# Scan in two buffers, zeros behind the weight chunks, and twelve of the modulation's parts moved from the scan into the context's attention

## The chip, the cores and the metric
The kernel runs on one core of a Trainium2 chip. The metric is the device time of one execution in microseconds. Engines are named PE (TensorE), VectorE (DVE), ScalarE (ACT), GpSimd (POOL) and SyncE (SP, which issues most DMAs).

## The reference
Two layers of a transformer block on 256 context and 256 latent tokens of width 1024, in float32. Cut to what matters here:

```python
for i in range(2):
    mod_x = split((silu(c) @ w_mod[i] + b_mod[i]), 6)      # shift, scale, gate: twice
    mod_c = split((silu(c_ctx) @ w_mod[i] + b_mod[i]), 6)
    u = concat([ada_norm(hc, g, mod_c[0], mod_c[1]), ada_norm(hx, g, mod_x[0], mod_x[1])])
    proj = u @ w_in[i]
    o_da  = diff_attention_mixer(proj[...])   # 4 heads, two softmaxes each, RoPE on the latent tokens
    o_ssd = ssd_mixer(proj[...])              # conv, chunked scan in both directions, gate, norm
    o_mla = mla_mixer(proj[...])              # 4 heads
    mix = concat([o_da, o_ssd, o_mla]) @ w_out[i]
    hc, hx = hc + mod_c[2] * mix_c, hx + mod_x[2] * mix_x
    ... # moe_ffn: 16 experts, top 2 of one group; hx and (in layer 0) hc are updated
return rms_norm(hx, final_norm_g)
```

A chunk of the scan (128 tokens) computes, for each direction and head, `y = ((C B^T) * exp(a_cum_i - a_cum_j) * mask) @ (x * dt) + exp(a_cum) * (C @ state)`, and adds `d_skip * x`.

## The kernel before, in words
Each engine runs one program of its own, in the order written, and the engines meet at semaphores. All loops over layers, tiles and heads are unrolled; only the expert loop is a loop on the chip. A tile is 128 tokens: tiles 0 and 1 are context, 2 and 3 latent. In layer 1 only tiles 2 and 3 go through scan and attention.

PE's order in a layer is: norm, input projection, states of the scan, rotation (RoPE), `scan_tiles`, `attention`, `out_projection`, router, experts. VectorE, ScalarE and GpSimd follow the same order.

`scan_tiles` before, for each tile i: PE multiplies C and B (`cb`, L612); GpSimd builds rows (`ew`, L1786), and PE spreads them over the partitions by a product with ones (L622, the cast) into PSUM banks 2 and 3, one direction after the other; VectorE subtracts and clamps (L1150, eight small operations, the clamp); ScalarE takes the exp (L1582); GpSimd multiplies by the masked scores (L1804), having made x*dt (L1792) and d_skip*x (L1797) for the tile; PE sums (L634 and L640) into banks 4 to 6; VectorE adds up and gates y (L1163 to L1174, the y chain); ScalarE takes its square and the root (L1584, L1510, L1511); VectorE norms it (L1182), PE transposes it (L402) and VectorE copies it out (L1187). `ew` is one buffer for each direction, so GpSimd builds the rows of a tile only when PE has summed the tile before (L1785).

The modulation is cut into 30 parts: for each of two layers three groups, in each four products with a chunk of w_mod of 2 MB (L424) and one part that turns the result (L402 on `modrow`). A part is placed wherever PE's program says `spare(n)`; VectorE has the same calls at its own places. Five parts run before the projections, five in the rotation and 20 in layer 0's scan (five for each tile: two behind each cast and one at the end). Bank 7 holds their sums. The chunks come through a ring of four slots of 2 MB in SBUF, together with w_in and w_out; SP loads a slot once its last user has released it (L1834). The order is: group 0, w_in's five, groups 1 to 5, w_out's two, then the experts' weights.

The experts' rows go through a DRAM tensor, `slots`, which must be zero before tokens are scattered into it. SP writes the zeros with four DMAs of 6 MB (L1898), before it loads w_in's chunk for z.

`attention` runs over units (kind, tile, head): 32 in layer 0, the first 16 of them context (256 keys), and 16 in layer 1 (512 keys). In step s PE makes the scores of unit s (L677 for `da`, L680 for `ml`), turns the probabilities of unit s-2 (L402) into bank 6 or 7, and multiplies unit s-3 with v (L705); VectorE takes maxima (L1213) and mixes the two softmaxes (L1222 to L1225), ScalarE the exp (L1600) and the copy of the turned probabilities (L1611).

Of the kernel before, what the change touches and what calls it, by code (L numbers as in the profile page):

```python
# [16 lines left out]
P = 128  # L17
DM = 1024
# [40 lines left out]
DEPTH_GROUPS = 3  # L59
MOD_PARTS = [(l, g, kk) for l in range(DEPTH) for g in range(DEPTH_GROUPS) for kk in range(5)]  # L60
# [120 lines left out]
def hybrid_dit_kernel(nc, consts, x, c, ctx, c_ctx, norm_mix_g, norm_ffn_g, w_mod, b_mod, w_in, w_out, da_lambda,  # L181
# [3 lines left out]
    with ExitStack() as stack:  # L185
# [66 lines left out]
        y_skip = take(512)  # L252
        sc = take(64 * 12).rearrange("p (k n) -> p k n", n=64)
# [93 lines left out]
        def ut_count(layer, t, half):  # L347

            return 2 * (TT * layer + t - FIRST_T[layer]) + half

# [28 lines left out]
        def _(pe):  # L379
# [226 lines left out]
            def scan_tiles(l):  # L606
                first = FIRST_T[l]
                for i, t in enumerate(range(first, TT)):
                    for g in range(2):
                        bank = open_bank(f"cb{l}{t}{g}")  # L610
                        r = slice(64 * g, 64 * g + 64)
                        last = nc.tensor.matmul(bank[:, 0:P], xbc[r, 4, P * t:P * t + P],  # L612
                                                xbc[r, 5, P * t:P * t + P], start=True, stop=True)
                        close_bank(last)
                    for d in range(2):
                        n = 2 * i + d

# [3 lines left out]
                        for b in range(2):  # L621
                            last = nc.tensor.matmul(ps[:, 2 + b, :], ones[:, :],   # L622
                                                    ew[:, d, 4 * b:4 * b + 4, :].rearrange("p h i -> p (h i)"),
                                                    start=True, stop=True)
                        last.then_inc(S("rows_cast", l), 1)
                        spare(2)
# [4 lines left out]
                    for d in range(2):  # L631
                        pe.wait_ge(S("w_ready", l), 2 * i + d + 1)
                        for hh in range(SSD_H):
                            last = nc.tensor.matmul(ps[:, 4, 64 * hh:64 * hh + 64], ew[:, d, hh, :],  # L634
                                                    xdt[:, d, 64 * hh:64 * hh + 64], start=(d == 0 and hh == 0),
# [7 lines left out]
                    if i > 0:  # L643
                        y_transposes(l, t - 1, i)
                    spare(1)
# [8 lines left out]
            def attention(l):  # L654
# [3 lines left out]
                for s in range(len(units) - DA_H + LAG_TURN + 1):  # L658
# [9 lines left out]
                    if s < len(units):  # L668
# [13 lines left out]
                        last.then_inc(S("scores_done"), 1)  # L682
                    n = s - 2
                    if 0 <= n < len(units):
# [5 lines left out]
                        if n >= 2:  # L690
                            pe.wait_ge(S("probs_t_ready"), before + n - 1)
                        for k in range(nk // P):
                            last = tr(ps[:, 6 + n % 2, P * k:P * k + P], probs[:, n % 3, 0, P * k:P * k + P])
# [222 lines left out]
        def _(dve):  # L916
# [218 lines left out]
            def scan_tiles(l):  # L1135
                first = FIRST_T[l]
                for i, t in enumerate(range(first, TT)):
                    if i:
                        dve.wait_ge(S("w_ready", l), 2 * i)
                    for g in range(2):  # L1140
                        bank = claim(f"cb{l}{t}{g}")
                        for d in range(2):
                            last = tt(gm[:, d, g, :], bank[:, 0:P], tri[d], ALU.mult)
                        emptied(last)
                    for d in range(2):
                        n = 2 * i + d
                        dve.wait_ge(S("rows_cast", l), n + 1)
                        for hh in range(SSD_H):

                            last = ts(ew[:, d, hh, :], ps[:, 2 + hh // 4, P * (hh % 4):P * (hh % 4) + P],  # L1150
                                      sc[:, 8, 32 * d + 8 * t + hh:32 * d + 8 * t + hh + 1], 0.0, ALU.subtract,
                                      ALU.min)
                        last.then_inc(S("decay_clamped", l), 1)
# [17 lines left out]
                    dve.wait_ge(S("skip_ready", l), i + 1)  # L1171
# [766 lines left out]
```

## Time and profile before

| | us |
|---|---|
| median of 3 runs (lowest, highest) | 1500.27 (1499.72, 1504.12) |
| the profiled execution | 1498.55 |
| its span | 1496.4 |
| PE busy in the span | 1226.1 (82%) |
| VectorE busy | 465.7 (31%) |
| ScalarE busy | 264.9 (18%) |
| GpSimd busy | 121.3 (8%) |
| DMA, mean over the span | 232 GB/s |

The span runs from the first to the last instruction of the profiled execution. Busy times are summed over the whole span and say nothing of a stage; the stages are read from stretches of it. Layer 0's scan lies at about 240 to 327 us, its attention from there to 426, its experts from 534 to 820; layer 1's scan at 1016 to 1059 and its attention to 1120. The granted clock is given as a share of 2.4 GHz.

### The profile page before, as it was taken

The page shows a single profiled execution, that of the slowest core. Times are in us where ns is not written, and L with a number is a line of the kernel's source. Part 1 is how long each engine was busy: PE and PEld are TensorE (multiplying, and loading weights), DVE is VectorE, ACT ScalarE, POOL GpSimd, SP SyncE. Part 2 cuts the span into 40 slices and gives each one's busy share as a digit, 9 for nine tenths or more (in the row PEclk, how much of TensorE's full clock was granted, in tenths as well). Part 3 has the DMA queues.
Part 4 walks back from the last instruction along what each step waited for, and adds up shares of the span by engine and source line. Part 5 has one row for each costly group of instructions (what it writes and reads, how often), then busy time and mean ns, then how long its engine had stood idle before and what let it go on. Part 6 is the DMA issues. An engine that isn't in the chain of part 4 may idle for free.

```text
span 1496.4 us, 13900 instructions
## 1 busy us (share of the span) xinstructions
PE 1226.1 (82%) x5162; PEld 562.9 (38%) x5162; DVE 465.7 (31%) x1088; ACT 264.9 (18%) x564; POOL 121.3 (8%) x107
## 2 busy tenths in 40 slices
PE   3899887879998379999897299976798399788792
PEld 1363333346653123333232146533466133222231
DVE  2311444656732501111011621465562311001014
ACT  1320101114521311111010322101242111001002
POOL 2000021640000200000000200033100100000001
PEclk9899999995799689999999599986599699899995
DMA  9998109990021399999999310023003599999942
GB/s 348 379 353 310 56 0 383 420 376 2 1 74 39 161 315 378 386 382 378 388 427 339 112 56 1 0 87 137 0 8 161 188 374 387 397 402 389 424 185 91
DMA packets 86029, 347.83 MB, mean 232 GB/s; under 512 B 5958, under 2 KB 37387, under 8 KB 63435
## 3 DMA queue, kind: packets, MB, share of 16 engines
q1 hardware_dynamic: 67056, 308.76, 53.5%
q10 hardware_dynamic: 14907, 24.70, 5.0%
q0 software_dynamic: 4000, 13.49, 2.6%
q8 instruction: 41, 0.67, 0.2%
q14 instruction: 25, 0.20, 0.0%
HBM read 302.89 MB, written 44.04 MB: 232 GB/s over the span
## 4 chain that ended last, share of the span: by engine, by line
PE 64%; DMA 16%; DVE 13%; issue 3%; ACT 2%; POOL 1%; ACTq 1%; SPq 0%; POOLq 0%; DVEq 0%
PE ps L801 17%; PE ps L459 11%; DMA ring<-in_exp_w_up 8%; PE ps L822 7%; PE ps L726 6%; PE ps L468 5%; PE ps L402 4%; DMA ring<-in_w_mod 3%; DMA arena<-in_exp_w_up 3%; PE ps L705 2%; PE ps L424 2%; PE ps L634 1%; PE ps L680 1%; PE ps L622 1%; PE ps L677 1%
## 5 line engine op out<-in xcount | busy, mean ns | idle before, releaser
L801 PE MATMUL ps<-ring,arena 128*64 128x512 f32 x1024 | 235.3, 613 | 26.9 <-DMA ring<-in_exp_w_up 26.9
L402 PE MATMUL ps<-cst,arena 128*128 128x128 f32 x594 | 109.8, 319 | 93.6 <-DMA arena<-slots 37.4
L459 PE MATMUL ps<-u,ring 128*128 128x512 f32 (+1 forms) x416 | 168.8, 566 | 10.0 <-ACT u L1537 6.2
L1422 DVE TENSOR_TENSOR arena<-arena,ps 128x256 f32<-128x256 f32 x44 | 26.8, 610 | 421.1 <-ACT arena L1662 421.1
L402 PEld LDWEIGHTS ps<-cst,arena 128*128 128x128 f32 x594 | 76.1, 162 | 179.7 <-issue 62.3
L801 PEld LDWEIGHTS ps<-ring,arena 128*64 128x64 f32 x1024 | 72.5, 141 | 167.6 <-issue 139.1
L459 PEld LDWEIGHTS ps<-u,ring 128*128 128x128 f32 x416 | 80.2, 195 | 97.3 <-issue 91.1
L822 PE MATMUL ps<-arena 128*64 128x512 f32 x512 | 115.4, 592 | 0.9 <-ACT arena L1666 0.9
L801 PE MATMUL ps<-arena 128*64 128x512 f32 x384 | 91.7, 633 | 15.2 <-DMA arena<-in_exp_w_up 15.2
L726 PE MATMUL ps<-u,ring 128*128 128x512 f32 (+1 forms) x256 | 83.1, 486 | 1.0 <-DVE u L1266 1.0
L468 PE MATMUL ps<-ring,u 128*128 128x256 f32 (+1 forms) x224 | 75.4, 496 | 6.9 <-DVE arena L1129 6.9
L1662 ACT ACTIVATE arena<-ps 128x256 f32<-128x256 f32 x44 | 16.9, 384 | 341.7 <-PE ps L801 341.7
L424 PE MATMUL ps<-ring,cond 128*32 128x512 f32 x384 | 50.6, 661 | 19.2 <-DMA ring<-in_w_mod 19.2
L1430 DVE COPY arena<-ps 128x512 f32<-128x512 f32 x44 | 30.4, 692 | 110.4 <-PE ps L822 110.4
L822 PEld LDWEIGHTS ps<-arena 128*64 128x64 f32 x512 | 36.5, 137 | 73.5 <-issue 72.1
L726 PEld LDWEIGHTS ps<-u,ring 128*128 128x128 f32 x256 | 48.5, 190 | 34.9 <-issue 30.1
L1762 POOL DMA_INDIRECT arena<-slots,slot_ids x12 | 12.1, 1010 | 591.1 <-ACTq L1698 588.0
L468 PEld LDWEIGHTS ps<-ring,u 128*128 128x128 f32 x224 | 44.0, 199 | 36.6 <-issue 33.3
L1600 ACT ACTIVATE arena<-ps,arena 128x512 f32<-128x512 f32 (+1 forms) x72 | 43.9, 614 | 63.0 <-DVE arena L1214 63.0
L801 PEld LDWEIGHTS ps<-arena 128*64 128x64 f32 x384 | 27.9, 145 | 70.6 <-issue 54.7
L705 PE MATMUL ps<-arena 128*128 128x64 f32 x320 | 51.0, 308 | 1.9 <-ACT arena L1611 1.9
L705 PEld LDWEIGHTS ps<-arena 128*128 128x128 f32 x320 | 50.0, 234 | 2.9 <-ACT arena L1611 2.8
(252 smaller groups left out, 1174.8 us busy)
## 6 DMA issues: line engine op xcount, KB each, us to landing
ring<-in_w_mod SPq DMA_DIRECT2D x24, 2048.0 KB, 14.9
ring<-in_exp_w_gate SPq DMA_DIRECT2D x22, 2048.0 KB, 23.2
ring<-in_exp_w_up SPq DMA_DIRECT2D x22, 2048.0 KB, 28.4
arena<-in_exp_w_down SPq DMA_DIRECT2D x22, 2048.0 KB, 22.2
slots<-zeros SPq DMA_DIRECT2D x4, 6144.0 KB, 41.0
arena<-in_exp_w_gate SPq DMA_DIRECT2D x10, 2048.0 KB, 22.8
arena<-in_exp_w_up SPq DMA_DIRECT2D x10, 2048.0 KB, 28.5
u<-in_exp_w_down SPq DMA_DIRECT2D x10, 2048.0 KB, 25.7
```

The costliest lines, as they stand in the source:

```text
L402: return nc.tensor.transpose(dst, src, ident[0:n, 0:n])
L424: last = nc.tensor.matmul(bank[32 * j:32 * j + 32, :], cond[:, k, :], w[:, k2, 512 * j:512 * j + 512], start=(k == 0), stop=(k == 7), tile ...
L459: last = nc.tensor.matmul(bank[row:row + width, 0:T - c0], w[:, k, n:n + width], u[:, k, c0:T], start=(k == 0), stop=(k == KT - 1))
L468: last = nc.tensor.matmul(bank[:, i * width:(i + 1) * width], u[:, k, P * t:P * t + P], w[:, k, n:n + width], start=(k == 0), stop=(k == K ...
L705: last = nc.tensor.matmul(ps[:, g % 2, 64 * hh:64 * hh + 64], probs_t[:, n % 2, k, :], v[:, k, 64 * hh:64 * hh + 64], start=(k == 0), stop ...
L726: last = nc.tensor.matmul(bank[:, 0:T - c0], w[:, k, P * m:P * m + P], u[:, k, c0:T], start=(k == 0), stop=(k == KT - 1))
L801: last = nc.tensor.matmul(ps[BLOCK * half:BLOCK * half + BLOCK, 2 + b % 2, :].rearrange("p (s n) -> p s n", s=2), x_k, pair[:, :, a:a + 25 ...
L822: last = nc.tensor.matmul(ps[BLOCK * half:BLOCK * half + BLOCK, 6 + b % 2, :], hid_t[:, f % 2, BLOCK * (f // 2):BLOCK * (f // 2) + BLOCK], ...
L1422: tt(hid.rearrange("p (j c) -> p c j", j=2), silu_g.rearrange("p (c j) -> p c j", j=2), ps[:, 2 + b % 2, 256:512].rearrange("p (c j) -> p ...
L1430: v.tensor_copy(y_sb[:, b % 2, :], ps[:, 6 + b % 2, :]).then_inc(S("y_ready", l), 1)
L1600: last = a(probs[:, s % 3, m, 0:nk], ps[:, 2 + 2 * (s % 2) + m, 0:nk], ACT.Exp, scale=DA_SCALE if kind == "da" else MLA_SCALE, bias=nb[:, ...
L1662: a(silu_g, ps[:, 2 + b % 2, 0:256], ACT.Silu).then_inc(S("silu_done", l), 1)
```

## The change
The scan gets a second set of buffers for odd tiles: `ew` in the free rows of `u` (k = 0, 1 and 6, 7), the masked scores in `rt`, x*dt of direction 0 in `b_tok`. The rows, casts, clamps and exps of tile i+1 are put ahead of the sums of tile i on every engine, and the transposes of tile i-1 stand between the casts and the sums. In the scan a cast is followed by one part of the modulation instead of two and there is none at the tile's end, so the scan has 8 parts instead of 20. The other 12 run in layer 0's attention, one in each of steps 2 to 13; while context units run, the probabilities are all turned into bank 6, since bank 7 is the modulation's. The four zero DMAs move behind all weight chunks of layer 0, ahead of the experts' loads.

```diff
+MODS_LEFT = 12
+        ews = [[ew[:, d] for d in range(2)],
+               [u[:, k:k + 2, :].rearrange("p k t -> p (k t)").rearrange("p (h i) -> p h i", i=P) for k in (0, 6)]]
+        gms = [gm, rt[:, 0:8, :, :].rearrange("p s t e -> p (s t e)").rearrange("p (d g i) -> p d g i", d=2, i=P)]
+        def turned_probs(n, nk):
+            return ps[:, 6 if nk == NCTX else 6 + n % 2, :]
+        def mod_in_attention(layer, s):
+            return int(layer == 0 and 2 <= s < 2 + MODS_LEFT)
 # PE, scan_tiles
+                def cast_rows(i):
                     for d in range(2):
                         n = 2 * i + d
                         pe.wait_ge(S("rows_built", l), n + 1)
                         if n >= 1:
                             pe.wait_ge(S("decay_clamped", l), n)
...
                         last.then_inc(S("rows_cast", l), 1)
-                        spare(2)
+                        spare(1)
+                scores(0)
+                cast_rows(0)
+                for i, t in enumerate(tiles):
+                    if i + 1 < len(tiles):
+                        cast_rows(i + 1)
+                    if i:
+                        y_transposes(l, t - 1, i)
+                    if i + 1 < len(tiles):
+                        scores(i + 1)
                     if i == 0:
                         pe.wait_ge(S("states_done"), l + 1)
                     else:
                         pe.wait_ge(S("y_banks_read", l), i)
                     for d in range(2):
+                        pe.wait_ge(S("xdt_ready"), 2 * tiles_before(l) + 2 * i + d + 1)
                         pe.wait_ge(S("w_ready", l), 2 * i + d + 1)
...
-                    if i > 0:
-                        y_transposes(l, t - 1, i)
-                    spare(1)
 # PE, attention, step s
+                    spare(mod_in_attention(l, s))
...
-                        if n >= 2:
+                        if n >= 1 and units[n - 1][3] == NCTX:
+                            pe.wait_ge(S("probs_t_ready"), before + n)
+                            if nk > NCTX:
+                                pe.wait_ge(S("mod_placed"), DEPTH * DEPTH_GROUPS)
+                        elif n >= 2:
                             pe.wait_ge(S("probs_t_ready"), before + n - 1)
 # VectorE, scan_tiles
+                masked_scores(0)
+                for d in range(2):
+                    clamp(0, d)
+                    spare(1)
+                for i, t in enumerate(tiles):
                     for d in range(2):
...
+                        if i + 1 < len(tiles):
+                            clamp(i + 1, d)
                         if i and d == 0:
                             y_norm(l, t - 1)
-                        spare(2)
+                        if i + 1 < len(tiles):
+                            spare(1)
                     if i:
                         y_turned(l, t - 1)
-                    spare(1)
-
+                    if i + 1 < len(tiles):
+                        masked_scores(i + 1)
                     dve.wait_ge(S("y_summed", l), i + 1)
 # GpSimd
+                rows(0)
+                pool.wait_ge(filled, entry[f"state{l}{len(state_steps(l)) - 1}"] + 1)
+                x_dt(0, 0)
+                x_dt(0, 1)
+                skip(0)
+                pool.wait_ge(filled, max(entry[f"z{l}{t}"] for t in tiles) + 1)
+                rows(1)
+                weights(0)
+                x_dt(1, 0)
+                for i in range(1, len(tiles)):
+                    weights(i)
+                    pool.wait_ge(S("y_summed", l), i)
+                    x_dt(i, 1)
+                    if i + 1 < len(tiles):
+                        rows(i + 1)
+                        x_dt(i + 1, 0)
+                    pool.wait_ge(S("y_gated", l), i)
+                    skip(i)
 # SP
             for key in chunks:
-                if key == ("in", 0, "z", 0):
-                    sp.wait_ge(S("zeros_ready"), 1)
-                    ... (four DMAs of zeros)
                 load(ring_at[key], key)
...
+            sp.wait_ge(S("zeros_ready"), 1)
+            for k in range(ZERO_DMAS):
+                ... (the same four DMAs)
             experts(0)
```

## Rows read from the trace of the kernel before

**Rows 1.** Stretches (us): busy us and (instructions) by engine; PEclk, DMA share, GB/s.
```profile
257.00:327.00 70.00, 60.50 (x414) 30.92 (x411) 38.49 (x98) 10.00 (x18) 38.08 (x27) 0.98 0.98 394
343.00:371.00 28.00, 28.00 (x110) 21.84 (x109) 17.49 (x61) 12.73 (x48) 0.00 (x0) 0.50 0.00 1
391.00:423.00 32.00, 29.35 (x193) 21.08 (x192) 23.25 (x59) 18.79 (x48) 0.00 (x0) 1.00 0.00 1
1015.00:1059.00 44.00, 31.91 (x103) 19.21 (x104) 19.42 (x51) 5.45 (x8) 18.04 (x13) 0.62 0.16 68
```
**Rows 2.** Chain that ended last, layer 0's scan: start us, us, what.
```profile
237.07 18.27 DMA ring<-in_w_mod
...
261.79 0.63 PE ps L640 x4
...
274.68 3.57 PE ps L424 x32
...
282.74 0.63 PE ps L640 x4
...
296.18 4.65 PE ps L424 x32
...
326.26 0.63 PE ps L640 x4
...
328.95 1.21 DVE arena L1163 x2
...
334.47 0.49 DVE arena L1182
```
**Rows 3.** Timeline, PE: start us, us, line, operation, idle before and releaser.
```profile
264.47 1.98 PE L622 MATMUL ps<-arena,ones 128*128 128x512 f32 x4 [1.03 <-POOL arena L1786]
```
**Rows 4.** Single lines: count, duration in ns min/median/max, first and last start.
```profile
L1792 POOL TENSOR_TENSOR arena<-arena x12: 1042/1486/1492, 209.7 to 1041.6; 128x512 f32<-128x512 f32 x12
L1786 POOL TENSOR_TENSOR arena<-cst,arena x12: 1896/1899/2343, 200.0 to 1037.8; 128x1024 f32<-128x1024 f32 x12
L1168 DVE TENSOR_TENSOR arena<-arena x6: 692/1120/1189, 265.7 to 1062.4; 128x512 f32<-128x512 f32 x6
```
**Rows 5.** A stretch of two us, columns as in rows 1.
```profile
294.00:296.00 2.00, 2.00 (x4) 0.38 (x2) 0.00 (x0) 0.61 (x1) 1.25 (x2) 0.73 1.00 414
```
**Rows 6.** Chain that ended last, layer 0's attention, columns as in rows 2.
```profile
342.31 0.69 PE ps L402 x2
...
371.74 2.01 PE ps L677 x4
...
395.71 0.91 PE ps L680 x2
...
397.93 1.08 PE ps L677 x4
...
404.91 1.24 DVE arena L1213
...
408.30 1.14 DVE arena L1213
...
425.90 4.13 PE ps L726 x9
```
**Rows 7.** Chain that ended last, layer 1's scan.
```profile
1016.06 3.72 PE ps L622 x4
1019.81 2.17 DVE arena L1150 x8
...
1054.17 3.67 PE ps L634 x16
1057.84 1.16 PE ps L640 x4
```
**Rows 8.** Zero DMAs (columns of rows 4), DMA in attention (of 1), first expert matmuls.
```profile
L1898 SPq DMA_DIRECT2D slots<-zeros x4: 3824/17490/20381, 46.8 to 87.6; - x4
340.00:420.00 80.00, 76.78 (x352) 54.03 (x353) 56.42 (x159) 39.93 (x122) 0.00 (x0) 0.68 0.00 1
534.30 8.54 PE ps L801 x32
```

More of the change, by code:

```diff
@@ L606, in scan_tiles, with scores @@
             def scan_tiles(l):
-                first = FIRST_T[l]
-                for i, t in enumerate(range(first, TT)):
+                tiles = range(FIRST_T[l], TT)
+                def scores(i):
+                    t = tiles[i]
                     for g in range(2):
@@ L611, in scan_tiles @@
                         r = slice(64 * g, 64 * g + 64)
-                        last = nc.tensor.matmul(bank[:, 0:P], xbc[r, 4, P * t:P * t + P],
-                                                xbc[r, 5, P * t:P * t + P], start=True, stop=True)
-                        close_bank(last)
+                        close_bank(nc.tensor.matmul(bank[:, 0:P], xbc[r, 4, P * t:P * t + P],
+                                                    xbc[r, 5, P * t:P * t + P], start=True, stop=True))
+                def cast_rows(i):
                     for d in range(2):
@@ L1135, in scan_tiles, with masked_scores @@
             def scan_tiles(l):
[L1136 to L1139, printed above, removed]
+                tiles = range(FIRST_T[l], TT)
+                def masked_scores(i):
+                    if i >= 2:
+                        dve.wait_ge(S("w_ready", l), 2 * (i - 1))
                     for g in range(2):
-                        bank = claim(f"cb{l}{t}{g}")
+                        bank = claim(f"cb{l}{tiles[i]}{g}")
@@ L1142, in scan_tiles, with clamp @@
                         for d in range(2):
-                            last = tt(gm[:, d, g, :], bank[:, 0:P], tri[d], ALU.mult)
+                            last = tt(gms[i % 2][:, d, g, :], bank[:, 0:P], tri[d], ALU.mult)
                         emptied(last)
-                    for d in range(2):
[L1146 to L1153, printed above, removed]
+                def clamp(i, d):
+                    dve.wait_ge(S("rows_cast", l), 2 * i + d + 1)
+                    for hh in range(SSD_H):
+                        last = ts(ews[i % 2][d][:, hh, :], ps[:, 2 + hh // 4, P * (hh % 4):P * (hh % 4) + P],
+                                  sc[:, 8, 32 * d + 8 * tiles[i] + hh:32 * d + 8 * tiles[i] + hh + 1], 0.0,
+                                  ALU.subtract, ALU.min)
+                    last.then_inc(S("decay_clamped", l), 1)
@@ L1578, in scan, with decays @@
                 exp_and_ln()
-                for i in range(TT - FIRST_T[l]):
+                def decays(i):
                     for d in range(2):
                         act.wait_ge(S("decay_clamped", l), 2 * i + d + 1)
-                        a(ew[:, d, :, :], ew[:, d, :, :], ACT.Exp).then_inc(S("decay_exp", l), 1)
+                        a(ews[i % 2][d], ews[i % 2][d], ACT.Exp).then_inc(S("decay_exp", l), 1)
+                decays(0)
+                for i in range(TT - FIRST_T[l]):
+                    if i + 1 < TT - FIRST_T[l]:
+                        decays(i + 1)
                     act.wait_ge(S("y_gated", l), i + 1)
@@ L1780, in _, with rows @@
                         S("xde_ready", l), 1)
[L1781 removed]
+                tiles = range(first, TT)
+                def rows(i):
                     for d in range(2):
[L1784 to L1799 removed]
@@ L1800, in _, with skip, weights @@
+                def skip(i):
+                    g.tensor_tensor(y_skip.rearrange("p (m a n) -> p m a n", m=4, a=2), xs(tiles[i]),
+                                    xb(bcast[:, l, B_D:B_D + 8]), ALU.mult).then_inc(S("skip_ready"), 1)
+                def weights(i):
+                    pool.wait_ge(evacuated, entry[f"cb{l}{tiles[i]}1"] + 1)
                     for d in range(2):
```

57 lines of the change are left out of this document (27 added, 30 removed).

## The prediction, made before the changed kernel was run
> **What bounds the kernel now.** I read the page's slices first, then the busy shares of the stretches around the edit [rows 1], then the chain that ended last through layer 0's scan [rows 2], the durations of the scan's operations [rows 3, 4], the granted clock inside the scan [rows 5], the chain through both attentions and layer 1's scan [rows 6, 7], and the zero DMAs [rows 8]. The reader should see this. From 257 to 327 us (layer 0's scan) PE is busy 60.5 of 70 us while GpSimd is busy 38 and VectorE 38: no engine is full, the stage is a chain that goes round them. The 16 DMA engines are full there too (share 0.98), with the modulation's weights. The chain's first link is a transfer: PE stands until 255.3 for a chunk of w_mod. After that a tile's sums end at 262.4, 283.4, and the last one's at 326.9: 21.5 us a tile. From 343 to 371 us (context attention) PE never rests, but its clock is granted at 0.50 (the 1.2 GHz level), so its small matmuls set the pace; from 391 on it runs at 1.00. In layer 1 (1015 to 1059) the same scan has only two tiles, no modulation in it, and a mean clock of 0.62.
>
> **Start of layer 0's scan: nothing gained.** The rotation's five parts stay where they are, so the fourth chunk of the third group still lands at 255.3 [rows 2]. The new order places exactly four parts (two tiles' row casts, one each) before the first tile's sums, and the fourth of them needs that chunk. Tile 0's sums end at 263.0 instead of 262.4: +0.6 (scores of tile 1 now stand ahead).
>
> **Tiles 1 and 2.** Rows for tile i+1 go into the buffer that tile i-1 has just left, and PE casts them before it sums tile i. So one turn is: x*dt 1.49, first rows 1.90 (both GpSimd, after the sums) [rows 4], cast 1.98 [rows 3], clamp 2.17 [rows 7], cast 1.98, one chunk of modulation 1.79 (half of 3.57; the other part lies beside the clamp), transposes and scores together 1.1 (six small matmuls; an estimate from the 4 of 0.63 in [rows 2]), sums 5.1 (from 274.68 + 3.57 to 282.74 + 0.63) [rows 2], and some 0.7 of handing over. Sum 18.2 us. What leaves the path is the y chain on VectorE, one exp, one multiplication by the masked scores, and three of five modulation parts. Two tiles end at 299.4.
>
> **Tile 3.** There is nothing left to cast, but PE must transpose tile 2's y before it sums tile 3. In the last tile of before, sums end at 326.9, VectorE starts on them at 328.95 and has the norm at 334.96: 6.0 us [rows 2]. With 0.4 for sharing (below), 0.6 and 5.1: 12.3, so the last sums end at 311.7 at full clock, 15.2 us before 326.9.
>
> **The clock takes part of it back.** The turn now leaves PE without work for 3.5 to 4 us (x*dt and rows come first) and for over 6 us before tile 3. In the trace PE's clock fell between 294 and 296 (mean 0.73), after it had waited for a clamp, and two chunks took 4.65 instead of 3.57 (with the cast, my estimate is 1.6 in all) [rows 2, 5]. I count one such dip (1.6; between 0 and 10) and tile 3's sums at the lower level: 2 x (3.67 + 1.16) = 9.7 [rows 7] instead of 5.1, +4.6 (between 0 and 4.6). Net for the scan: -15.2 + 1.6 + 4.6 = -9.0. One more gain: before, tile 2's transposes and their copy stood between the last sums and VectorE's start on them (326.9 to 328.95); now they are over: -2.1. So attention starts 11.1 us earlier.
>
> **Sharing of GpSimd and VectorE.** y_acc + y_two takes 0.69 us alone and 1.12 at the median, beside GpSimd [rows 4]; the y chain meets GpSimd's x*dt and rows as it did before, so 0.4, between 0 and 1.5 a tile. The Trainium skill (SBUF — State Buffer, section "SBUF: two separate sides") says the pair of ports is an exclusive lock held for a whole instruction when VectorE reads two SBUF inputs. The trace agrees in kind (0.69 against 1.12); by the rule an addition could wait out a whole 1.90 us rows operation, about 1.2 more for each of two additions, 5 us over two tiles.
>
> **Twelve parts in the context attention.** Before, from the third step (342.3) to the first long one (371.7), 14 steps take 29.4 us at 0.50, 2.1 each [rows 6]. After, nine steps carry a chunk. At full clock such a step is half of 2.1-2.5 plus 1.86 (one chunk with its start), 3.05; three with a turn and two bare are near 1.9 (VectorE and ScalarE in a chain); sum 37. The first one or two chunks start at 0.50 and cost 1.8 more: 39, +9.5. The dense chunks should lift the clock, as the full-width casts do in the scan; if they didn't, nine chunks at 3.65 on top of 29.4 would give over 62, +33. Chunks must also arrive: five are still to load, 2 MB each, 5.3 us at 394 GB/s [rows 1], one released per step of 3: covered. The single turning bank lengthens nothing while a step is over 2 us. Only the chunk copies of VectorE (0.7, three) are new there, beside PE's work.
>
> **Latent part of attention.** It takes 54.2 us (371.7 to 425.9). Its first eight units ran mostly at 0.50 and took 26.2 (to 397.9). At full clock four are 3.4 (VectorE bound, 404.91 to 408.30) and four 2.2 (395.71 to 397.93): 22.5. -3.7, between 0 and -5.5.
> Layer 0: -11.1 + 9.5 - 3.7 = -5.3, say -5.5.
>
> **Layer 1, two tiles.** The first cast is still at 1016.1 and at 0.50. Casts and clamps of tile 0 end at 1027.9; tile 1's two casts and clamp take 6.1 to 9.6 more, scores 0.5 to 0.8, sums 5.1 to 9.7: 1039.8 to 1048.1. Then 6.0 to 6.9 for y and its norm, transposes 0.6 to 1.1, tile 1's sums 5.1 to 9.7: 1052 to 1066 against 1059.0, and 2.1 off behind it. Between -9 and +5; the second sums follow an idle stretch and are likely at 0.50, the first mixed: I take -1. Here the double buffer moves one serial wait in front of another, and buys little.
>
> **Zeros.** Four DMAs, 24 MB, now issue behind the last w_out chunk, near 355, with 3.8 to 20.4 us of SP's time each and some 65 us on the DMA engines [rows 8]. Behind them on SP are layer 0's first expert weights: issued near 415, needed when the expert matmuls begin at 534 [rows 8]. DMA is idle from 340 to 420 now (share 0.00) [rows 8], so this hides: 0. The scatter, some 20 us before the expert matmuls, waits for zeros that are done near 430. Without that slack it would cost up to 65. Taking them away from the first projections frees nothing: the page's chain of waits has no DMA there, and PE is full in those slices. Cost at nothing, between -1 and +3.
>
> **Sum.** -5.5 - 1 = -6.5 from the profiled execution's 1498.55 (span 1496.4 and 2.1 around it) gives 1492. That execution is 1.7 below the median of the three runs, so a like-for-like median would be 1494; I give 1492.5. The expert stages hang on the router and shift whole.
>
> **Rivals.**
> (B) The clock holds: no dip, tile 3 and layer 1's sums at full speed. For it: the mean from 257 to 327 is 0.98 in spite of waits in every tile [rows 1]. Against: over 6 us idle. Scan -6.2 more, layer 1 -4 more: 1482.
> (C) What the scan gives, attention takes: chunk steps at 3.4 instead of 3.05, latent steps VectorE-bound as before, layer 1 at +3. Layer 0 then gives -5.5 + 3 + 2 = -0.5; sum +2.5 on 1498.55, no change: 1501. For it: both the scan's PE work and attention's are PE-bound, and work only moves.
> (D) Slower: the scan at 0.50 from tile 1 on. Nine of the sixteen chunks between whose waits PE stayed at full clock are gone from it, and layer 1's scan without chunks has 0.62 [rows 1]. Each turn then pays 2 x 1.74 for casts, 1.8 for the chunk, 4.6 for the sums and 0.9 for the rest: 10.8, for both 21.6, less the 1.6 counted: +20. A cast lifts the clock for parts of a turn, as in layer 1, so three quarters of it, +15: 1507. It decides from +11 on, half of it; below that it only eats the gain. The Trainium skill (TensorE: Matmul & The Clock Gate, section "HAM oscillation — how this bites in real kernels") says that gaps between dense work throw the engine back to the lower clock again and again; the dip at 295 agrees.
> (E) Zeros or SP's late expert loads delay the scatter: 1500 to 1510; the slack of some 80 us speaks against it.
>
> **Chances.** Forecast 0.45, B 0.17, C 0.24, D 0.11, E 0.03. The forecast's own range is 1487 to 1497; the range for 8 in 10 takes in B and C: 1481 to 1504. A difference of 0.3% (4.5 us) is about what can be told from none. Faster: most of the forecast and B, 0.60; same: C and the forecast's edge, 0.27; slower: D, E and a little of C, 0.13.
>
> **What would show it.** Last layer 0 sums at 316 to 320, tile turns near 18 (21.5 before); PE's clock at 0.50 before tile 3's sums; context steps near 3.0 at clock 1.00; the out projection starting near 420; layer 1's last sums within 5 us of 1059 less the shift; zeros between 355 and 430 with the scatter not waiting. Wrong if turns stay at 21, if the clock is 0.50 through the context attention, or if the chunk DMAs stall PE there.

## The result and the profile after

The changed kernel takes 1510.29 us (median of 20 runs, 1502.18 to 1516.97), the kernel before 1502.01 (20 runs, 1497.21 to 1509.35): ratio 1.0052, 95% interval [1.0035, 1.0069]. It is slower by more than 0.3%; 1492.5 and "faster" had been forecast. The profiled execution took 1506.39 us, its span is 1504.3 (before: 1498.55 and 1496.4).

| us, from the chains of waits | before | after | difference | forecast |
|---|---|---|---|---|
| to the end of tile 0's sums, layer 0 | 262.4 | 264.8 | +2.4 | +0.6 |
| tiles 1 and 2 | 43.5 | 45.7 | +2.2 | -5.5 |
| tile 3 | 21.0 | 16.5 | -4.5 | -4.1 |
| last sums to attention's third step | 15.4 | 14.0 | -1.4 | -2.1 |
| third step to the first long unit | 29.4 | 36.9 | +7.5 | +9.5 |
| latent part of attention | 54.2 | 56.7 | +2.5 | -3.7 |
| out projection to layer 1's first cast | 590.2 | 593.4 | +3.2 | 0 |
| layer 1's scan (two tiles) | 42.9 | 44.0 | +1.1 | -1 |
| layer 1's attention | 60.9 | 56.7 | -4.2 | 0 |
| the rest | 376.5 | 375.7 | -0.8 | 0 |

The differences add up to the span's 7.9. In these two executions the scan gave nothing by its end (327.0 against 326.9) and attention paid 7.5 for the parts. Other traces below say how far to trust this. The last sums of the old scan with 20 parts end at 326.9, 328.8 (e1) and 329.1 (e14), those of the new scan at 327.0, 324.4 (e2), 325.0 (e8) and 324.3 (e13): over all of them the scan gave some 3 us, of the 9.0 forecast.

Stretches of the changed kernel, columns as in [rows 1]: the scan, the context attention, part of the latent attention, layer 1's scan, and the wait before its last sums.
```profile
257.00:327.00 70.00, 51.77 (x271) 32.16 (x270) 37.40 (x88) 8.94 (x17) 32.59 (x24) 0.77 0.49 196
341.00:377.00 36.00, 33.59 (x254) 17.05 (x255) 20.92 (x70) 13.97 (x49) 0.00 (x0) 0.99 0.98 383
383.00:403.00 20.00, 20.00 (x67) 13.14 (x66) 10.79 (x25) 7.31 (x20) 0.00 (x0) 0.50 1.08 381
1028.00:1072.00 44.00, 29.83 (x106) 17.75 (x108) 18.64 (x53) 5.45 (x8) 13.39 (x11) 0.62 0.06 27
1056.00:1070.00 14.00, 8.46 (x38) 7.69 (x39) 5.09 (x9) 1.22 (x4) 3.35 (x3) 0.50 0.00 0
```
In 70 us of scan PE is busy 8.7 us less than in [rows 1], and its clock fell from 0.98 to 0.77. The context attention, the other way round, now runs at 0.99 instead of 0.50.

The chain that ended last in layer 0's scan after the change (answers to [rows 2]): start us, us, what.
```profile
261.08 4.93 POOL u L1857 x4
266.01 1.00 POOL arena L1844
267.01 2.31 POOL arena L1838
269.37 3.80 PE ps L644 x4
...
281.11 0.48 PE ps L634 x2
...
302.61 1.93 PE ps L667 x16
...
305.69 3.60 PE ps L667 x16
309.29 1.18 PE ps L673 x4
```
Read it by turns. Tile 0's sums end at 264.8, but GpSimd is still multiplying tile 1's weights (L1857) until 266.0. The first cast (L644) takes 3.80, as at 1.2 GHz in [rows 7], instead of 1.98. The second bank of tile 2's scores (L634) waits behind VectorE's copies of the turned y (L1233). In the second turn tile 2's sums take 7.9 us (302.6 to 310.5) instead of 5.1, because the clock falls inside them.

Timeline of VectorE and GpSimd in the second turn: start us, us, engine, line, operation (other rows left out).
```profile
288.08 2.45 DVE L1214 TENSOR_TENSOR arena<-arena 128x512 f32<-128x512 f32 x1
288.09 4.20 POOL L1838 TENSOR_TENSOR u<-cst,arena 128x1024 f32<-128x1024 f32 x2
291.30 1.54 DVE L1218 TENSOR_TENSOR arena<-arena 128x512 f32<-128x512 f32 x1
292.26 1.49 POOL L1844 TENSOR_TENSOR arena<-arena 128x512 f32<-128x512 f32 x1
292.88 1.41 DVE L1220 TENSOR_TENSOR arena<-arena 128x512 f32<-128x512 f32 x1
294.21 2.15 DVE L1186 TENSOR_SCALAR u<-ps,arena 128x128 f32<-128x128 f32 x8
```
L1214 and L1218 (two inputs in SBUF) start beside a rows operation of GpSimd and end some 0.5 us after it has ended (rows end at about 290.05 and at 292.26); L1220 does the same behind x*dt, which ends at 293.75. The y chain takes 7.3 to 7.5 us in tiles 0 and 1, 4.2 in tiles 2 and 3, where GpSimd does nothing beside its additions. The clamp (L1186) is queued behind it: it could have started at 293.1, where the cast ended.

The same thing happens once more, outside the scan. GpSimd now builds tile 1's rows as soon as it has made `skip(0)`, which is while VectorE still rotates (RoPE). Timeline of VectorE and GpSimd in layer 1's rotation, after and then before:
```profile
1013.72 3.93 POOL L1838 TENSOR_TENSOR u<-cst,arena 128x1024 f32<-128x1024 f32 x2
1013.80 2.09 DVE L1090 TENSOR_TENSOR arena<-arena,cst 128x256 f32<-128x256 f32 x1
1015.92 2.00 DVE L1092 TENSOR_TENSOR arena<-arena 128x256 f32<-128x256 f32 x1
```
```profile
1005.08 0.41 DVE L1055 TENSOR_TENSOR arena<-arena,cst 128x256 f32<-128x256 f32 x1
1005.53 0.43 DVE L1057 TENSOR_TENSOR arena<-arena 128x256 f32<-128x256 f32 x1
```
Both operations are in the chain that ended last, and cost 3.3 us more there. This is about the whole of the +3.2 in the table's row "out projection to layer 1's first cast". It isn't chance: that stretch took 592.0 to 594.1 us in the profiled executions of all 12 kernels with the new order, and 588.8 to 590.2 in the four without it (before, e1, e3, e14). In layer 0 the same two operations take 1.22 and 2.00, and PE waits 1.0 us for them.

Context attention (answers to [rows 6]), layer 1's last tile ([rows 7]), and, from the issues' view, the zeros ([rows 8]).
```profile
350.98 1.85 PE ps L444 x16
...
354.09 1.90 PE ps L444 x16
356.00 14.42 DMA ring<-in_w_mod
370.47 1.93 PE ps L444 x16
```
```profile
1062.66 3.31 PE ps L667 x16
```
```profile
L1975 SPq DMA_DIRECT2D slots<-zeros x4: 3862/17634/20429, 368.3 to 409.5; - x4
```
A context step is a chunk (1.85), a turn, a product with v and the scores: 3.1 us, as forecast. (Eight of attention's nine chunks lie behind the third step's landmark; the first, at 1.2 GHz, falls into the table's row "last sums to attention's third step".) The 14.42 of DMA is the chain's way of naming a chunk that landed last; of that, PE stood still 1.4 us ahead of 370.47, and worked for the rest.

### The profile page after: what moved, and what is told of

Same layout as the page of the kernel before. It is cut to its first block, busy times and chain, and to the rows that moved or that the text cites. A ratio compares the mean times of both kernels' runs of the same rounds, so it can differ in the third digit from the quotient of the medians.

```text
span 1504.3 us, 13905 instructions
## 1 busy us (share of the span) xinstructions
PE 1229.3 (82%) x5162; PEld 558.7 (37%) x5162; DVE 473.9 (32%) x1088; ACT 265.9 (18%) x564; POOL 119.8 (8%) x107
## 4 chain that ended last, share of the span: by engine, by line
PE 63%; DMA 15%; DVE 14%; issue 2%; ACT 2%; POOL 1%; ACTq 1%; SPq 0%; POOLq 0%; DVEq 0%
PE ps L836 17%; PE ps L479 11%; DMA ring<-in_exp_w_up 8%; PE ps L857 7%; PE ps L761 6%; PE ps L488 5%; PE ps L422 4%; DMA arena<-in_exp_w_up 3%; DMA ring<-in_w_mod 2%; PE ps L444 2%; PE ps L644 2%; PE ps L667 2%; PE ps L740 2%; PE ps L710 1%; DVE arena L1259 1%
## 5 line engine op out<-in xcount | busy, mean ns | idle before, releaser
L836 PE MATMUL ps<-ring,arena 128*64 128x512 f32 x1024 | 240.9, 625 | 23.1 <-DMA ring<-in_exp_w_up 23.1
L1714 ACT ACTIVATE arena<-ps 128x256 f32<-128x256 f32 x44 | 16.9, 384 | 340.3 <-PE ps L836 340.3
L836 PEld LDWEIGHTS ps<-arena 128*64 128x64 f32 x384 | 27.8, 144 | 67.5 <-issue 54.3
L1259 DVE TENSOR_REDUCE arena<-ps 128x2 f32<-128x1024 f32 (+3 forms) x48 | 39.5, 822 | 32.9 <-PE ps L710 25.7
L740 PE MATMUL ps<-arena 128*128 128x64 f32 x320 | 45.4, 285 | 1.9 <-ACT arena L1663 1.9
## 6 DMA issues: line engine op xcount, KB each, us to landing
ring<-in_exp_w_up SPq DMA_DIRECT2D x22, 2048.0 KB, 27.4
```

Source lines behind the costliest of these rows:

```text
L740: last = nc.tensor.matmul(ps[:, g % 2, 64 * hh:64 * hh + 64], probs_t[:, n % 2, k, :], v[:, k, 64 * hh:64 * hh + 64], start=(k == 0), stop ...
L836: last = nc.tensor.matmul(ps[BLOCK * half:BLOCK * half + BLOCK, 2 + b % 2, :].rearrange("p (s n) -> p s n", s=2), x_k, pair[:, :, a:a + 25 ...
L1259: link(v.tensor_reduce(mx[:, s, 0:nm], ps[:, pair:pair + nm, 0:nk], AX.X, ALU.max))
```

## The experiments

All ratios are to the kernel before, from runs on the same chip; they are not exactly ratios of the medians, and two kernels are compared by their ratios where they ran on different chips. Single executions of one kernel spread by 10 to 15 us, and a stage of one profiled execution by several (the latent part took 51.8 to 58.7 us in kernels with parts in the context attention before it), so verdicts rest on ratios, and landmarks only say where.

**e1, zeros only** (the kernel before with the four DMAs moved behind the weight chunks).

> The kernel before with one edit: the four zero DMAs behind the weight chunks. Theory T (the loss is made in the scan's turn and in the context attention, the zeros are free): ratio to before 1.000, within 0.3%; the first expert matmuls at 534, with layer 0's out projection at 426. Rival Z (the zeros now collide with the attention's chunk loads and hold up the experts' weights on SP): 5 to 8 us slower, and the stretch from the out projection to the first expert matmuls grows from 108 us.

Measured 0.9997 [0.9979, 1.0014]. The zeros are free.

**e2, the changed kernel with the zeros back at their old place.**

> The changed kernel with the zero DMAs back at their old place. T: as slow as the changed kernel, 7 to 9 us above before; turns of the scan still 22 and 24 us. Z: within 2 us of before.

Measured 1.0071 [1.0055, 1.0087]: no gain from putting them back. The loss is in the two other edits, the scan's buffers and the moved parts.

**e3, parts only** (one buffer, as before; 8 parts in the scan, 12 in attention).
```diff
-                        spare(2)
+                        spare(1)
...
+                    spare(mod_in_attention(l, s))
```

> The kernel before (one buffer, zeros in the old place) with 12 modulation parts moved from the scan to the context attention. T: a tile of the scan loses one part from its path (-1.8 each, last sums near 320 instead of 327), the context attention gains 7 to 9.5 us (36 to 39 instead of 29.4 from its third step to the first long one), latent part -4 to +2: total 0 to +5 us. Rival A (the parts are covered in attention): context attention at most +3, total -4 to -8 us.

Measured 1.0019 [1.0002, 1.0036]. Tile ends 258.1, 278.9, 300.3, 323.9: with 12 parts fewer the scan ends 3.0 us sooner, and attention takes 10.6 more from the last sums to the first long unit (55.4 against 44.8). Two stretches of its scan, columns as in [rows 1]:
```profile
257.00:285.00 28.00, 22.39 (x100) 11.78 (x101) 17.04 (x38) 3.33 (x6) 19.15 (x13) 0.74 0.67 261
285.00:325.00 40.00, 30.37 (x159) 15.84 (x157) 18.76 (x56) 6.67 (x12) 19.27 (x15) 0.84 0.43 159
```
The parts taken out had stood beside waits, and with them went the full clock (0.98 in [rows 1]). e2 and e3 differ by the scan's two buffers and their order alone, and ran together: 1.0071 [1.0055, 1.0087] against 1.0019 [1.0002, 1.0036]. So the double buffer itself costs 6 to 8 us on top of the parts.

**e4, the 12 parts behind the tiles' sums** (three a tile, none in attention; `spare(3)` after `y_summed`, on VectorE after the y chain).

> The changed kernel, but the 12 parts stand behind each tile's sums in the scan (three each), where TensorE now waits for rows, and none in attention. T: the context attention goes back to about 29.4 us (-7.5 against the changed kernel), the clock stays up in the turns (-3 to -5), three parts of 1.85 overrun the gap of 3.3 to 4.6 by 1 to 2 us a turn: 5 to 9 us faster than the changed kernel, near before or 2 below. Rival Q (the turn is set by GpSimd and VectorE, so what is put on TensorE costs nothing, but attention's start at half clock is what counts): 8 to 12 faster. Rival P (every part costs its full 1.85 wherever it stands): no faster than the changed kernel.

Measured 1.0113 [1.0086, 1.0140], a miss: turns of 31.9 us. Its chain, second turn:
```profile
269.40 2.27 DVE arena L1221
271.67 0.11 DVE mod L982
271.82 5.96 PE ps L445 x32
```
A chunk that follows a turning part waits until VectorE has placed the result, and VectorE comes to that (L982) only after the y chain; then two chunks at 1.2 GHz (L445) stand ahead of the cast. The gap is there, but not where these parts can use it.

**e5, rows held** (GpSimd waits for `y_gated` before x*dt and rows, so that it doesn't run beside the y chain).
```diff
                     pool.wait_ge(S("y_summed", l), i)
+                    pool.wait_ge(S("y_gated", l), i)
                     x_dt(i, 1)
```

> The changed kernel, GpSimd starts x*dt and the next rows only when VectorE has gated y. Theory L (VectorE's additions of two SBUF tensors wait for whole GpSimd operations, and the next clamp is queued behind them): the y chain falls from 7.3-7.5 to 4.2 us in tiles 0 and 1, its additions to 0.69 us each, the rows take 1.90; the first clamp of the next tile starts 9.5 instead of 7.5 us after the sums, so a turn is 1 to 3 us longer and the kernel 2 to 6 us slower. Rival N (the chain is long for another reason, as the wait for d_skip*x): the chain stays over 6 us.

Measured 1.0111 [1.0083, 1.0139]. Its chain, first turn:
```profile
264.89 0.70 DVE arena L1214
...
267.89 1.04 POOL arena L1844
268.93 1.86 POOL arena L1838
270.84 3.80 PE ps L644 x4
```
The mechanism stands: alone, the additions take 0.70 and the chain 4.2, and one rows operation 1.86 instead of 2.31. As a remedy it fails: the turn grows to 27.4 us. GpSimd's work is on the path and starts 4.4 us after the sums instead of 1.2, and at the turn's end the sums fall to 1.2 GHz (7.9 us instead of 5.1). That fall wasn't in the expectation, and the kernel loses 9 us to the changed one where 2 to 6 were expected.

**e6, three parts behind tile 2's sums, nine in attention.**

> The changed kernel with three of attention's twelve parts put behind tile 2's sums, where TensorE waits 6 us for the norm. Theory C (a part costs nothing where TensorE waits and about 3 us in a context step, and work there keeps the clock up for tile 3's sums): 9.3 -> 5.1 to 7 us for tile 3's sums, three context steps 1.9 us shorter; 6 to 10 us faster than the changed kernel, equal to before or 2 below. Rival (the parts overrun the wait and the clock falls all the same): 2 to 4 us faster only.

Measured 1.0023 [1.0003, 1.0044]. Ahead of the last sums:
```profile
314.29 3.64 PE ps L445 x16
...
318.97 1.91 PE ps L668 x16
```
That is some 4 us under the changed kernel, not the 6 to 10 of theory C and close to the rival. The sums (L668) are at full speed, but the third part, again held by the placing of the one before it, runs at 1.2 GHz and overruns.

**e7, early scores and rows.** PE makes the scores of tile i+1 before its casts, VectorE their masks before the clamps, GpSimd the rows before x*dt.
```diff
                     pool.wait_ge(S("y_summed", l), i)
-                    x_dt(i, 1)
                     if i + 1 < len(tiles):
                         rows(i + 1)
+                    x_dt(i, 1)
+                    if i + 1 < len(tiles):
                         x_dt(i + 1, 0)
```

> The changed kernel with two orders changed in the scan: the scores of tile i+1 (and their masking) come before its casts, and GpSimd builds the next rows before x*dt of the tile at hand. Theory L+O (the turn is y chain, clamp, cast, clamp, sums, with 1.2 us lost to the scores' second bank behind VectorE's copies): rows and first cast 1.0 us earlier but hidden behind the y chain, 1 to 2 us a turn from the scores: 2 to 4 us faster than the changed kernel. Rival (rows bound the turn): 4 to 7 us faster.

Measured 1.0023 [1.0005, 1.0041]; turns 21.4, 18.6, 16.6, last sums at 320.8 instead of 327.0. The first turn's two casts still run slow (3.4 and 3.8 us); in the second they take 1.98 and 1.95. So nearly the forecast turn (18.6 for 18.2) exists where the wait for the copies is gone and the clock holds.

**e8, twelve products in layer 1's gap** (128x512, they compute nothing of the output, between the two tiles' sums).
```diff
+                    if l == 1 and i == 0:
+                        for _ in range(12):
+                            nc.tensor.matmul(ps[:, 7, :], ones[:, :], h[:, 0, :], start=True, stop=True)
```

> The changed kernel with 12 extra products of 128x512 into the free bank 7, in layer 1 between tile 2's and tile 3's sums; they change no result. Theory K (the sums of the last tile take 9.3 instead of 5.1 us only because TensorE's clock falls in the wait before them): layer 1's last sums at 5.1 to 6 us, last sums to first sums 12 to 13 instead of 17.5 us, kernel 3 to 4 us faster than the changed one. Rival (the clock falls whatever is run there, or the products overrun the wait): no gain, up to 2 us slower.

Measured 1.0040 [1.0017, 1.0064]. The products (10.50 us) end 4 us after the norm is ready; the sums behind them take 5.0 instead of 9.3.

**e13, the same with six products.**

> The changed kernel and nothing else but six products of 128x512 between the two tiles' sums of layer 1's scan (there were twelve in the run with 1.0040, and their end held up the sums). Theory T: layer 1's second sums take 5.1 us and start when the norm is there, 3 to 4 us less than the changed kernel: ratio to before 1.001 to 1.004. Rival I (the products give 9 us by themselves, by what they do to the clock later): ratio 0.996 to 1.000. Rival N (no effect): 1.005 to 1.007.

Measured 1.0010 [0.9995, 1.0025]: against the changed kernel's 1.0052 [1.0035, 1.0069] some 5 to 6 us, give or take 3. In its trace the stretch from the end of layer 1's first sums to the end of its last takes 12.7 instead of 17.5 us, which is nearly all of that. Last sums of layer 1 in e8 and then in e13:
```profile
1051.60 10.50 PE ps L678 x24
...
1062.53 1.73 PE ps L667 x16
```
```profile
1059.93 1.73 PE ps L667 x16
```

**e9, the two buffers alone** (20 parts in the scan, two a cast and one behind each tile's sums; old zeros).

> The scan's two buffers with all 20 parts of the modulation left in the scan (two behind each cast, one behind each tile's sums) and the zeros where they were before; the attention is that of before. In the kernel before, the DMA engines are full through the scan (share 1.01 from 257 to 310) and a chunk of 2 MB takes 5.3 us of them, so a tile with four chunks can't turn in less than 21.3 us, and it turned in 21.5. Theory T (the double buffer alone can't shorten the scan, since the chunks' transfers bound it; that is why parts had to move, and they take from the attention what they gave): last sums of layer 0 at 326 to 332, the first long attention step within 3 us of that of before less their shift (371 to 376), layer 1 as in the changed kernel (+1 to +5 to the last sums), ratio to before 1.000 to 1.005. Rival R (the additions that wait for GpSimd set the turn whatever PE and the DMA engines do): turns of 22 to 24, last sums at 333 or later, ratio 1.005 to 1.010. Rival A (the two costs of the changed kernel add up: parts alone gave 1.0019, all of it 1.0052 to 1.0071): scan alone 1.003 to 1.005 with the last sums near 330.

Measured 1.0155 [1.0125, 1.0184], worse than every theory. Its chain:
```profile
253.41 17.91 DMA ring<-in_w_mod
...
278.84 1.90 PE ps L444 x16
...
289.70 3.52 PE ps L444 x16
```
Tile 0's sums now stand behind eight parts and wait for their seventh chunk; they end at 278.8. Then VectorE copies the group's sums (after the chunk at 278.84) before it starts y, and another chunk, at 1.2 GHz (289.70), stands ahead of the second cast: turns of 27. So with this placement the double buffer needs parts moved (other placements of all 20 weren't tried), and moved parts cost attention what e3 shows.

**e10, e7 with two parts (a chunk, a turn) behind tile 2's sums, ten in attention.**

> The changed kernel with the scores of tile i+1 and their masks ahead of its casts, GpSimd's rows ahead of x*dt (as in the run with 1.0023), and in addition two of the twelve parts (one chunk and one turn) behind tile 2's sums; ten stay in attention. Theory T (tile 3's sums run at 1.2 GHz because PE has stood idle for the y chain before them, and a chunk there costs nothing): tile 3's sums take 5 to 7 us instead of 9.3, attention is 1 to 2 us shorter, last sums of layer 0 at 317 to 320, ratio to before 0.998 to 1.001. Rival: the chunk runs at 1.2 GHz (3.6 us) and the clock falls again before the sums: ratio 1.001 to 1.003.

Measured 1.0001 [0.9980, 1.0022]. The ratio is T's, the mechanism isn't: the last sums (L667) are still at 1.2 GHz.
```profile
311.35 3.31 PE ps L667 x16
...
315.82 3.60 PE ps L667 x16
```

**e11, e10 with six products in layer 1's gap.**

> The kernel of the run before, with six products of 128x512 that compute nothing of the output between the two tiles' sums of layer 1's scan. Theory T: layer 1's second sums take 5.1 instead of 9.3 us without being held up, 2 to 4 us less than the run before: ratio to before 0.996 to 0.999. Rival: six aren't enough to keep the clock (or they run at 1.2 GHz and end late), and the ratio is within 0.001 of the run before.

Measured 0.9928 [0.9904, 0.9952], 9 to 11 us under e10 and more than the 4.4 us that the last sums gain in its trace. Its profiled execution was the longest of the seven (1503.5 us, granted clock 0.888 over the whole span) and doesn't show where the rest comes from; the six others took 1488.0 to 1494.8 us at 0.894 to 0.899, e10's twelve had 0.881 to 0.891. That points to the clock, in a stretch that no trace of this kernel shows. The spread of the executions goes the same way: the changed kernel's 20 run from 1502.2 us at 0.885 to 1517.0 at 0.875.

**e12, e11 with eight more products in layer 0.**
```diff
+                    if l == 0 and i == 2:
+                        pe.wait_ge(S("decay_clamped", l), 8)
+                        for count in (6, 2):
+                            spare(1)
+                            for _ in range(count):
+                                nc.tensor.matmul(ps[:, 2, :], ones[:, :], h[:, 0, :], start=True, stop=True)
```

> The kernel with early scores, early rows, ten parts in attention and six products in layer 1's gap, and in addition eight products of 128x512 that compute nothing of the output in layer 0 behind tile 2's sums (six behind the chunk, two behind the turning part). Theory T (the clock falls because PE stands idle, and each last tile's sums at 1.2 GHz cost 4.2 us): tile 3's sums take 5.1 instead of 9.3 us, last sums of layer 0 at 314 to 318, ratio to before 0.988 to 0.993, some 3 us under the kernel without the eight. Rival R (the 0.9928 was a chance of the chip's clock in those executions): ratio 0.996 to 1.000. Rival S (the clock, held here, is given back in the attention, which has started at 1.2 GHz in nearly every trace): tile 3's sums at 5.1 and the attention no sooner by as much; ratio within 0.002 of 0.9928.

Measured 0.9912 [0.9883, 0.9941]: 1487.68 us against 1501.91, the fastest here, faster than both kernels. Its chain behind tile 2's sums:
```profile
302.62 1.85 PE ps L445 x16
304.47 5.35 PE ps L684 x12
...
310.25 1.72 PE ps L684 x4
...
312.41 1.73 PE ps L667 x16
```
The products (L684) make the last sums start 1 us later than in e10 and take 5.0 instead of 9.3: 317.3 against 320.6. Whether that adds to e11 in the median (0.9928 and 0.9912, intervals overlap) isn't settled. Layer 1's attention, from its last sums to its end, in e10, in e12 and in the changed kernel:
```profile
1058.00:1119.00 61.00, 52.35 (x255) 34.05 (x252) 41.38 (x100) 27.87 (x73) 0.00 (x0) 0.74 0.00 1
```
```profile
1050.00:1107.00 57.00, 45.95 (x255) 30.59 (x253) 41.80 (x101) 27.83 (x73) 0.00 (x0) 0.85 0.00 1
```
```profile
1072.00:1129.00 57.00, 47.84 (x254) 30.85 (x255) 41.72 (x101) 27.86 (x73) 0.00 (x0) 0.82 0.00 1
```
In e12 the same 255 matmuls take 6.4 us less of PE than in e10. But the changed kernel, without any product, is as short. In every trace the clock is at 1.2 GHz some 5 us after the last sums at the latest, and the attention's length follows how long that lasts: until 21 us after the last sums in the changed kernel, e11 and e12 (56.7 us), 26 in e13 (58.7), 28 before (60.9), 30 in e8 (twelve products) and in e7 and e10 (61.2), 35 in e2 (63.2). That products shorten the attention behind them isn't shown.

**e14, products in layer 1's scan of the kernel before** (six behind tile 0's sums, ten behind the last cast).

> The kernel before (one buffer, 20 parts in the scan), with products of 128x512 that compute nothing of the output in layer 1's scan: six behind tile 0's sums, ten behind the last cast. In the kernel before, layer 1's casts take 3.10 to 3.72 us, the second tile's sums 4.83 and the attention behind it 60.9 us, at a mean clock near 0.7. Theory T (the clock alone gives most of it): the second tile's first cast takes 2 us, its sums 2.6 for each direction instead of 4.8, layer 1's last sums come 3 to 5 us sooner and its attention takes 57: ratio 0.993 to 0.997. Rival W (the products gain only where the two buffers have left nothing but PE's own work behind the gap): ratio 0.998 to 1.001. Rival O (they overrun and hold up the casts): 1.001 or more.

Measured 1.0012 [0.9991, 1.0033]. Both sets overrun, as in rival O, though the interval reaches into W's. Six products at 1.2 GHz for the most part take 7.8 us and hold up the first cast until 1044.2, when its rows had been ready at 1040.2. The ten:
```profile
1050.42 8.58 PE ps L608 x20
1059.00 1.73 PE ps L640 x16
```
A product takes 0.86 us at full clock, so ten of them end at 1059.0, where GpSimd had the weights ready at 1056.3. The attention behind them takes 62.5 us, not the 57 of theory T. Whether fewer would help the single-buffer scan wasn't tried.

## Why the prediction was wrong

**What failed is the step "tiles 1 and 2: 18.2 us a turn".** Measured 21.9 and 23.7, 9.2 us over the two, of which the forecast had 1.6 as "one dip"; "wrong if turns stay at 21" came true. The two turns together took 44.3 to 45.7 us in four traces of this scan (e2, e8, e13 too), but what fell to 1.2 GHz differs: in e2 they are 24.3 and 20.7. By its own terms:

| us | forecast | tile 1 | tile 2 |
|---|---|---|---|
| sums to the second cast | 7.5 and handing | 10.7 | 9.8 |
| second cast and chunk | 3.8 | 3.8 | 3.8 |
| transposes and scores | 1.1 | 2.3 | 2.3 |
| sums | 5.1 | 5.1 | 7.9 |

- The clock, 5.7: the first cast +1.8 and +1.1, the second turn's sums +2.8. (The 1.1 would have given nothing by itself, since the clamp behind that cast waits for the y chain in any case.) I had counted one dip at the price of the one in [rows 5]. Taking chunks out of the scan and putting x*dt and rows ahead of the cast makes a dip in each turn. That rival D named this and priced it at up to 21.6 was right in kind: the clock fell in parts of a turn, not from tile 1 on.
- Transposes and scores, 2.4: I took them as six small matmuls with nothing between. The second bank of scores waits for VectorE's copies of the turned y. That wait was to be read from the order in the diff. e7 takes it away.
- GpSimd late by 1.2 in the first turn: tile 1's weights are queued ahead of x*dt and rows. Not in my sum.
- VectorE beside GpSimd, 1.1 on the path, in the second turn. I took 0.4 a tile, from the median of L1168 [rows 4]. The y chain grew by 3.2 us a turn (7.4 against 4.2); most of it lies beside the rows and the cast, and only the clamp queued behind it reaches the path. The Trainium skill (SBUF — State Buffer, section "SBUF: two separate sides") gives the shared pair of ports to one side for a whole instruction, where VectorE has two inputs in SBUF. The timeline and e5 agree, and the growth is more than the 2.4 I had worked out by that rule.

These come to 10.4 for 9.2: x*dt took 1.0 instead of 1.49, and the handing over less than the 0.7 counted.

**A term that the sum put at nothing: layer 1 up to its first cast, 3.3.** "The first cast is still at 1016.1" took the rotation as it was. But the new order puts GpSimd's rows beside it, and two operations of VectorE take 4.0 us instead of 0.8. I had asked what GpSimd meets only inside the scan. Unlike the turns' losses, this one shows in every kernel with the new order, e12 too; no run held these rows back.

**Parts right.** Tile 3 (12.3 + 4.6 = 16.9; measured 16.5, its sums at 1.2 GHz; the four terms named for 12.3 add up to 12.1). The copy off the path (-2.1; -1.4 measured). The zeros (0; e1). Chunk steps in context attention (3.05; 3.1, at clock 0.99) and the whole price of the parts (+9.5; +7.5 here for eight chunks, +10.6 in e3 from the last sums). The lift of the clock by the chunks, half of what that price rested on, came as told.

**The latent part failed too:** -3.7 forecast, +2.5 measured. The clock that the chunks lift to 0.99 falls back to 0.50 once they end (383 to 403). The size of it is chance: this stretch took 51.8 to 58.7 us in eleven kernels with parts in the context attention, six of them at 54.3 or less, and 53.4 to 54.3 in the five without. What is shown is that no gain of 3.7 came.

**Start and layer 1.** Of the +2.4 at the start 0.6 was forecast, by a path that wasn't the one: PE waits for no chunk before tile 0's sums, and stands for the four casts and the clamps between them. The rotation begins 1.6 us later than before, which is mostly the execution's (1.0 later in e1, 1.2 in e3), and takes 1.0 longer beside GpSimd's rows. Layer 1's scan (+1.1) is in the range given (-9 to +5) and, as feared, trades one wait for another; its sums are at 1.2 GHz behind 7 us of PE idle. The price of that was the larger surprise: six products that only keep the clock give 5 to 6 us (e13) and, with e7's order, 9 to 11 (e10 to e11). The Trainium skill (TensorE: Matmul & The Clock Gate, section "HAM oscillation — how this bites in real kernels") describes clocks lost in gaps between dense work. The runs agree: behind that gap the sums take 9.3 us, and 5.0 with products in it. Layer 1's attention (-4.2, forecast 0) is the execution's luck, as e12's comparison shows.

**Where the expected gain went:** of the 15.8 us that the three turns were to give at full clock, 2.3 came. The clock took 10 (5.7 in tiles 1 and 2, 4.2 in tile 3's sums), waits that the new order made some 3.5; the later start took the 2.3, attention 7.5 for the parts, and layer 1's rotation 3.3. Rival D (slower, 1507, chance 0.11) came nearest, in part by luck: of its 15 us of clock beyond the forecast the two turns show some 4, and the rest of the miss is from terms that it didn't have. e3 (1.0019) and the whole (1.0052 to 1.0071) say that the two buffers on top of the moved parts make it worse, not better. e11 and e12 say that the new scan, with its order mended and the clock held, is faster than the kernel before. How much of that is the two buffers' own isn't shown, since no run has well-sized products in the single-buffer scan.

## What to carry over

Work moved out of a gap takes the clock with it: before moving filler out of a stage that waits, price every matmul left in it at both levels of the clock, gap by gap. With a double buffer, redraw each engine's queue: what now stands ahead of the operation on the path (copies, a chain that another engine's operations lengthen, a small part's result). Do it for the stage ahead as well: work that may start earlier will, beside whatever runs there. Filler can be products of no use, but only as many as fit, at their measured price.

## What was not expected of the hardware

- In the changed kernel's scan a VectorE addition of two 128x512 SBUF tensors (0.69 us alone) took 1.4 to 2.45 us beside GpSimd's tensor_tensor operations, and each time ended about 0.5 us after the GpSimd operation did; that operation lengthened too (1.86 to 2.31). In the rotation operations of 0.41 to 0.43 us took 2.0. VectorE's operations that read one input from PSUM (L1215, 0.69; L1089, 0.42) kept their times.
- Keeping the clock through a 7 us gap shortened the 9.3 us of sums behind it to 5.0. In the attention that follows, the clock was at 1.2 GHz in every trace, with products and without, and came back 21 to 35 us after the last sums; what sets that time isn't shown.
